# A gate chunk of the input projection, moved from the chunked scan to the front, by thirds of tokens among the norm steps

## What is computed

```
h = RMSNorm(x);  u = h @ w_in         # z | x,B,C | dt | q,k,v | z_att | q_mem | z_mem | gates 3 x 1024
A: causal conv, SiLU, 16-head state-space scan in chunks of 128 tokens, gated RMSNorm
B: three groups of dilated windowed attention, merged by their softmax denominators
C: attention into 256 memory tokens;  K, V = RMSNorm(mem) @ w_mem_kv
y = RMSNorm(x + (sigmoid(gate_i) * (branch_i @ w_i), summed over i) @ w_out)
```

## Time and profile before

| | us |
|---|---|
| median of 3 runs | 2109.82 (2109.42 to 2115.62) |
| the profiled execution | 2112.42, its span 2110.6 |
| TensorE busy, matmuls | 1979.0 (94%), 14301 instructions |
| VectorE, ScalarE, GpSimd busy | 985.8, 765.1, 242.0 |
| mean granted clock of TensorE | 0.965 |
| moved by DMA | 257.18 MB, mean 122 GB/s |

### The profile page before, as it was taken

The page is one execution under the profiler, slowest core; times in us unless marked ns, Lnnn a source line. Parts: engine busy times, 40 slices in busy tenths (PEclk is TensorE's granted clock), DMA queues, the critical chain, the costliest instruction groups (busy, mean ns, idle before and its releaser), DMA issues.

```text
span 2110.6 us, 34859 instructions
## 1 busy us (share of the span) xinstructions
PE 1979.0 (94%) x14301; PEld 1892.0 (90%) x14301; DVE 985.8 (47%) x1941; ACT 765.1 (36%) x1642; POOL 242.0 (11%) x358
## 2 busy tenths in 40 slices
PE   5999999999989999999999899999999669969997
PEld 5899999999989999999999889669999659969997
DVE  5303676535465354443337684013555455454523
ACT  5223444323353333332655223115556532133202
POOL 1000111100001010112212100001211111100000
PEclk9999999999999999999999999998999879989999
DMA  6311332311112121212256784764545635554422
GB/s 216 92 42 52 93 93 83 93 46 40 49 33 65 41 67 39 87 44 90 86 170 198 237 260 141 268 228 134 169 153 161 216 88 179 175 173 140 143 84 104
DMA packets 171742, 257.18 MB, mean 122 GB/s; under 512 B 20229, under 2 KB 115269, under 8 KB 171557
## 3 DMA queue, kind: packets, MB, share of 16 engines
q1 hardware_dynamic: 149328, 187.97, 28.4%
q0 software_dynamic: 22256, 66.98, 9.4%
HBM read 188.13 MB, written 66.76 MB: 121 GB/s over the span
## 4 chain that ended last, share of the span: by engine, by line
PE 85%; DVE 5%; ACT 4%; DMA 3%; issue 2%; SPq 0%; POOL 0%; DVEq 0%; ACTq 0%; POOLq 0%
PE bank L2296 21%; PE bank L2297 21%; PE bank L2298 21%; PE bank L2496 3%; PE bank L2469 2%; PE bank L2452 2%; PE bank L2711 2%; PE bank L2600 1%; PE bank L2430 1%; DVE w_lo L1762 1%; PE bank L2755 1%; PE bank L2533 1%; DMA sums<-sum_T 1%; PE bank L2395 1%; PE bank L2394 1%
## 5 line engine op out<-in xcount | busy, mean ns | idle before, releaser
L2296 PE MATMUL bank<-w_hi,hT_hi 128*128 128x256 f32 (+1 forms) x1848 | 536.9, 291 | 0.2 <-issue 0.2
L2297 PE MATMUL bank<-w_lo,hT_hi 128*128 128x256 f32 (+1 forms) x1848 | 524.6, 284 | 0.0
L2298 PE MATMUL bank<-w_hi,hT_lo 128*128 128x256 f32 (+1 forms) x1848 | 523.6, 283 | 0.0
L2296 PE MATMUL bank<-hT_hi,w_hi 128*128 128x352 f32 x1344 | 451.3, 336 | 6.3 <-DVE acc L2143 5.7
L2298 PE MATMUL bank<-hT_hi,w_lo 128*128 128x352 f32 x1344 | 439.1, 327 | 0.0
L2297 PE MATMUL bank<-hT_lo,w_hi 128*128 128x352 f32 x1344 | 438.8, 327 | 0.0
L2296 PEld LDWEIGHTS bank<-w_hi,hT_hi 128*128 128x128 f32 (+1 forms) x1848 | 349.8, 189 | 1.9 <-issue 0.5
L2298 PEld LDWEIGHTS bank<-w_hi,hT_lo 128*128 128x128 f32 (+1 forms) x1848 | 350.6, 190 | 0.6
L2297 PEld LDWEIGHTS bank<-w_lo,hT_hi 128*128 128x128 f32 (+1 forms) x1848 | 349.7, 189 | 1.3
L2296 PEld LDWEIGHTS bank<-hT_hi,w_hi 128*128 128x128 f32 x1344 | 257.8, 192 | 20.1 <-issue 8.6
L2297 PEld LDWEIGHTS bank<-hT_lo,w_hi 128*128 128x128 f32 x1344 | 258.8, 193 | 0.5
(11 more groups left out here) (423 smaller groups left out, 2934.6 us busy)
## 6 DMA issues: line engine op xcount, KB each, us to landing
w_raw<-in_w_in SPq DMA_DIRECT2D x96, 512.0 KB, 5.0
kvring<-in_cache_win_kv SPq DMA_DIRECT2D x98, 256.0 KB, 4.8
feat_T<-fstage POOLq DMA_DIRECT2D x40, 528.0 KB, 4.2
fstage<-feat_T SPq DMA_DIRECT2D x16, 528.0 KB, 4.2
xc<-feat_T SPq DMA_DIRECT2D x8, 1024.0 KB, 5.9
sums<-sum_T SPq DMA_DIRECT2D x32, 256.0 KB, 4.5
o_rows<-obuf POOLq DMA_DIRECT2D x48, 132.0 KB, 2.0
mo<-o_rows SPq DMA_DIRECT2D x24, 264.0 KB, 3.3
```

The lines of the kernel that those rows point to most:

```text
L2296: pe.matmul(out, xh(k), wh(k), start=(k == 0), stop=False)
L2297: pe.matmul(out, xh(k), wl(k), start=False, stop=False)
L2298: ins = pe.matmul(out, xl(k), wh(k), start=False, stop=(k == nk - 1))
```

## The change

Chunk `front_gate` (gate features 22 and 23, the last gate chunk of the scan) becomes chunk 1, between mk0 and mk1. Its six thirds are laid into the table `between` and the steps behind it, by thirds of tokens: `G(f, j)` waits until the norm steps that hold its third are in `hT_lo`. mv0, chunk 3, takes slot 0 instead of 1, so that mk1, mv0 and mv1 follow mk0 in slot 0 while the gate chunk keeps slot 1. The squares go to `soft` instead of `fstage`, which now takes the gate's features. The scan has five gate chunks over its 31 places instead of six.

```diff
-    mem_chunks = [chunk("mk", i, "w_mem_kv", CW * i) for i in range(2)]
+    front_gate = ("feat", FT_GATE + 6, "w_in", C_GATE + 3 * CW)
+    mem_chunks = [chunk("mk", 0, "w_mem_kv", 0)]
+    g0 = chunk(*front_gate)
+    mem_chunks += [chunk("mk", 1, "w_mem_kv", CW)]
...
+    gates.remove(front_gate)
...
+    G = lambda f, j: ("feat", g0, f, j)
     between = {2: [("load0", 0)], 3: [("split0", 0)], 4: [("low0", 0), ("load0", 1), T(k0, 0)], 5: [T(k0, 1), E(k0, 0), ("split0", 1)],
-               6: [("low0", 1), E(k0, 1), T(k1, 0)], 7: [turn(k0), T(k1, 1), E(k1, 0)], 8: [E(k1, 1), ("turned", k0), ("split", k0)],
-               9: [L(k0), ("dt_w",), T(v0, 0), turn(k1)],
-               10: [("norm_h", 10), ("norm_l", 9), ("norm_l", 10), ("turned", k1), T(v0, 1), E(v0, 0), ("split", k1), L(k1), E(v0, 1)]}
+               6: [("low0", 1), ("load0", 2), E(k0, 1), G(0, 0)], 7: [turn(k0), G(1, 0), ("split0", 2)],
+               8: [("turned", k0), ("low0", 2), ("load0", 3), T(k1, 0)],
+               9: [T(k1, 1), E(k1, 0), E(k1, 1), ("split0", 3), ("dt_w",), G(0, 1)],
+               10: [("norm_h", 10), ("norm_l", 9), ("norm_l", 10), turn(k1), ("low0", 3), ("load0", 4), G(1, 1)]}
...
-    sched += [T(v1, 0), T(v1, 1), E(v1, 0), ("split", v0), L(v0), ("dt",), E(v1, 1), ("split", v1), L(v1), ("dt_out",)]
+    sched += [T(v0, 0), ("turned", k1), T(v0, 1), E(v0, 0), E(v0, 1), G(0, 2), ("split0", 4), ("low0", 4), G(1, 2), ("split", v0)]
+    sched += [T(v1, 0), T(v1, 1), E(v1, 0), L(v0), ("dt",), E(v1, 1), ("split", v1), L(v1), ("dt_out",)]
...
-        xsq = fwide[:, 0, 0:D]
+        xsq = soft[:, 0, :, :].rearrange("p h c -> p (h c)")
...
+        def wslot(n):
+            return 0 if n == 3 else n % 2
...
-                    act.wait_ge(s_pj, chunk_end[n - 2])
-                act.activation(w_hi[:, n % 2, :, :], w_raw[:, :, :], ACT.Copy).then_inc(s_whi, 1)
+                    act.wait_ge(s_pj, chunk_end[max(x for x in range(n) if wslot(x) == wslot(n))])
+                act.activation(w_hi[:, wslot(n), :, :], w_raw[:, :, :], ACT.Copy).then_inc(s_whi, 1)
...
+                        if n == 1:
+                            pe.wait_ge(s_hlo, 2 * (2 + -(-THIRD * (j + 1) // P)))
```

More of the change, by code:

```diff
@@ L709, in third_parts @@
             return parts
+        def wslot(n):
+            return 0 if n == 3 else n % 2
         def feat_done_stores(k):
             return 16 * (k // 2)
-        n_qz = 2 * MH
+        n_qz = 2 + 2 * MH
         def qz_stored(eng):
@@ L981, in acc_of @@
             return (acc0, acc1)[ft % 2]
-        raw_gates = [chunks[s[1]][1] + s[2] for s in sched[sched.index(("ssd_dA",)):] if s[0] == "feat" and s[3] == 2]
+        raw_gates = [FT_GATE + 6, FT_GATE + 7] + [chunks[s[1]][1] + s[2] for s in sched[sched.index(("ssd_dA",)):] if s[0] == "feat" and s[3] == 2]
         gate_no, n_sig = {}, 0
@@ L1761, in split_lo @@
                 dve.wait_ge(s_whi, n + 1)
-                dve.tensor_tensor(w_lo[:, n % 2, :, :], w_raw[:, :, :], w_hi[:, n % 2, :, :].bitcast(F32),
+                dve.tensor_tensor(w_lo[:, wslot(n), :, :], w_raw[:, :, :], w_hi[:, wslot(n), :, :].bitcast(F32),
                                   ALU.subtract).then_inc(s_wlo, 1)
@@ L2321, in blocks_behind_perm @@
                         out = bank[u % 3][:, 0:CW]
-                        pe.matmul(out, xh, w_hi[:, n % 2, k, :], start=(k == ks[0]), stop=False)
-                        pe.matmul(out, xh, w_lo[:, n % 2, k, :], start=False, stop=False)
-                        ins = pe.matmul(out, xl, w_hi[:, n % 2, k, :], start=False, stop=(k == ks[-1]))
+                        pe.matmul(out, xh, w_hi[:, wslot(n), k, :], start=(k == ks[0]), stop=False)
+                        pe.matmul(out, xh, w_lo[:, wslot(n), k, :], start=False, stop=False)
+                        ins = pe.matmul(out, xl, w_hi[:, wslot(n), k, :], start=False, stop=(k == ks[-1]))
                         if k == ks[-1]:
@@ L2370, in _ @@
                     n = s[1]
-                    slot = n % 2
+                    slot = wslot(n)
                     u = proj[s]
```

## The result

The kernel after takes 2135.35 us (median of 4 runs, 2134.58 to 2138.8), the kernel before 2109.62 beside it (2105.28 to 2115.62): ratio 1.0132, 95% interval 1.0111 to 1.0153. It is slower, by 25.7 us in the medians.

What follows compares the result with a forecast made beforehand. TensorE, busy 94% of the span, was taken as the bound. Front +28.5 and scan +2.4 (1.0 - 15.4 + 13.5 + 3.3) gave +30.9: 2143.3 us profiled, 2141 median, range 2131 to 2150, with neighbours 2117 to 2154.

Steps and rivals of the forecast that it cites:

- the likeliest case: Whole kernel: the main forecast of a slower kernel, 2141 us, own range 2131 to 2150, chance 0.50.
- The front, +28.5: Front up to the dt step: it starts at 101.4 instead of 72.9, from 23.2 of work plus waiting and clock.
- The replay: Front's norm steps and projections replayed instruction by instruction with the thirds added, giving 15.5 us of TensorE waiting.
- Removed, -15.4: Scan: of the six thirds taken out, four really save time, 3.86 us each.
- the third that saves nothing, +1.0: Scan, ahead of the first `L2711`: two thirds instead of three save nothing, and `L2711` ends 1.0 later.
- The new waits, +13.5 and +3.3 of clock: Scan steps 4 and 5: `w_hi` ahead of `xtok` delays `Lm`, 6 and 7.5 us, plus 3.3 of lost clock.
- That third saves nothing either: Scan, step 6, where TensorE waits 12.4 us on late weights: the third removed there saves zero.
- Behind step 6 the program is the same: Rest of the kernel after the scan's step 6: no change in time was charged.
- the scan gives its four thirds: Rival, chance 0.15: weights land in time, no new wait in the scan; +14.1 in all, 2124 us.
- the hole is filled: Rival, chance 0.10: thirds fill the front's 10.5 us of waiting; front +8 to +13, scan -23.2, 2095 to 2100 us.

Runs made afterwards that it cites:

- e2: Kernel after, front only: evictions of three gate thirds put behind the next norm step's square and root on ScalarE; 2130.06 us, ratio 1.0098.
- e9: Kernel before, chunk kept in the scan: three thirds ahead of the first `L2711`, five in each of five steps, eight in step 6; 2096.78 us, ratio 0.9930.
- e1: Kernel after, scan only: load and `w_hi` of two gate chunks put behind `xtok` and the following third in steps 4 and 5; 2121.98 us, ratio 1.0056.
- e6: Kernel after: two weight loads issued before the step's `sums` instead of behind, ScalarE's order unchanged; 2126.01 us, ratio 1.0067.
- e7: Kernel before: load and `w_hi` behind the last gate chunk moved behind part 5 of step 6, `low` into step 7; 2099.11 us, ratio 0.9943.
- e4: Kernel after with the moved chunk also left in the scan, so computed twice; 2135.69 us, ratio 1.0127.
- e3: Kernel before with the gate chunk taken from the scan and run behind the front's last projection chunks, six thirds on end; 2132.75 us, ratio 1.0104.
- e5: Kernel after with the edits of e1 and e2 together; 2112.41 us, ratio 1.0013.
- e10: e7 with the decay tiles of step 7 put behind attention outputs 4 and 5; 2090.51 us, ratio 0.9928.
- e12: e9 with the edit of e10, the decay tiles of step 7 behind attention outputs 4 and 5; 2085.35 us, ratio 0.9898.
- e8: e5 plus the edit of e7, on the kernel after; 2105.9 us, ratio 0.9995.

## Why the prediction was right, and where its sizes were off

The direction, the place of both costs and the likeliest case held: 2141 forecast, 2135.35 measured. The forecast was +30.9 between the profiled executions; +22.7 was measured there, and +25.7 between the medians, because the profiled execution of before was 2.8 us above its median.

**The front, +28.5.** Measured +28.6 at the mark (+30.2 at the dt step). The replay's waits were 2.1, 3.9, 2.0, 1.9 and 0.9; measured were 1.97, 3.76, 0.83, 1.94 and 0.82. The replayed root of step 7 at 48.1 came at 48.27. That the roots wait behind the thirds' evictions is shown by e2, where moving the evictions gives 9.5 us. That the sum agrees to 0.1 is luck in part: the waits were 1.4 us less than replayed (14.1 for 15.5), at the dt step the clock cost 3.4 us where the sum had 0.3, and 1.6 came back behind it. (The replay writes 344 columns for a third's matmul; it has 352, and its 0.29 is the value for 352.) By the Trainium skill ("TensorE: Matmul & The Clock Gate", opening table of specs) ScalarE takes its queue strictly in order; e2 agrees, where the root of step 7 comes at 41.49 once no eviction stands ahead of it, and at 48.27 with one.

**Removed, -15.4, and the third that saves nothing, +1.0.** Both held. In e9 the four steps with a sixth third before are 3.86 us shorter each, and in e1 the three of them that hold no slow `L2719`. Over the first `L2723` the offset grew by 0.9: it started 0.7 earlier and took 1.6 longer, where 0.9 and 2.0 were summed.

**The new waits, +13.5 and +3.3 of clock.** 16.8 forecast, 6.9 + 8.9 = 15.8 measured: 11.8 of waiting and 4.0 of clock. The size of the delay held, but not the wait in which it shows: the sum had TensorE come to `L2723` too early for `Lm`, and it waited before that, for `yy` and for an eviction that `w_hi` held up on ScalarE, and only 0.4 for `Lm`. e1 shows that they are `w_hi`'s place, e6 that it is the late load behind the `sums` and not the copy. That the load ahead of step 4 lands earlier since it goes ahead of `zt` was put at 1.5: it landed 20.6 us behind the end of `L2723`, the other 22.3. The rule of the Trainium skill ("Trainium Kernel Development and Optimization", Key Constraints: all queues share 16 DMA engines) would have had no difference; the two loads read different tensors, so this does not decide it.

**The term that was off: "That third saves nothing either".** The third at the hole of step 6 was put at zero. The stretch there took 31.6 us instead of 34.5: -2.9. The load on which the hole hangs (e7) took 10.15 us in the kernel after and 12.65 in the kernel before, and was issued 0.4 earlier in the step; in both, and in e1 to e6, `w_hi` starts 6.60 us before the `L2711` line. So the sum was right that the third is cover there and the load sets the end. But the landing goes with the third: 12.65 and 12.74 us in the two kernels that have it (before, e4), 9.86 to 11.57 in the six that do not (after, e1, e2, e3, e5, e6), and their stretches take 31.1 to 33.9 against 34.5 and 34.2. Why is not shown, so "nothing" is not shown either.

**"Behind step 6 the program is the same".** It is, but it took 2.9 us less: the stretch shown at e1 took 23.0 instead of 26.9, at a clock of 0.93 instead of 0.81, and 1.0 came back elsewhere. Between front and scan another 1.3 went, with the same program. These three, 2.9 + 2.9 + 1.3, and 1.0 of the new waits are 8.1 of the 8.2 us between 30.9 and 22.7. They are small terms that the trace of before could not give; none turns the argument.

**The rivals.** That the scan gives its four thirds was false in this order and true in e1. That the hole is filled was false in this order and a little true in e2's: with the evictions behind the roots the chunk costs 19.1 for 23.2 of work. e5 is what both together give, 2112, which is no gain either: I had this rival at 2095 to 2100, because I let the thirds fill the whole 10.5 us and the scan return all six.

## What to carry to other kernels

Before work is moved into a wait, read what the wait's engine queue would hold afterwards: here evictions of 0.46 us ahead of a root cost 9.5 us in three places, because each waited for a whole block of matmuls, and the clock fell with the waits. Where fewer blocks stand in a step, everything that is counted in blocks drifts against the step; look at each load and copy whose place comes from such a count, and see which one now stands in front of the chain. And take the holes that are there first: a load that comes late ahead of `xtok`, as in the change's two new waits, was in step 6 of the kernel before as well, and mending it (e7) and the order of the attention outputs (e10, e12) made a faster kernel; the move did not. The root behind a projection's eviction is in the front of before too (46.68 and 46.96); no run mended it there.

## What the runs showed that was not expected

- The same stretch of the same program gets a different clock from kernel to kernel: 0.81 in before and 0.80 in e1 against 0.93 in after for the same matmuls behind step 6, 26.9 and 26.2 us against 23.0; in the front, four kernels with one order of work (e1, after, e4, e6) stood at +28.0, +28.6, +28.8 and +30.7 at the mark; e4 falls from +28.8 there to +24.0 at the scan's start; e8 and e5 differ by 0.09 for 90 us behind step 6. A gain of 17.2 us at step 6 became 13.1 at the end that way. For an edit worth less than 4 us the trace, read up to the place of the edit, tells more than the time.
- The first `L2711` of the scan, behind a wait of 1.4 us, took 5.07 us; behind one of 4.2 (the wait for `Lm` in the kernel after) 6.64, and in e1, behind 4.75, 7.09, where full clock is 3.52. In the kernel after that wait of 4.2 us costs another 4.9 in the 40 matmuls behind it (6.64 + 3.52 instead of 3.52 + 1.78).
- The landing of one load of weights, issued at the same place of step 6, took from 9.86 us (e1) to 12.74 (e4) in eight kernels.
